# One expert at a time on both column halves of TensorE, with 4 MB weight loads and sums kept in PSUM, in the expert layer of a one-layer diffusion backbone

## The reference, cut to what matters

```python
combine = jnp.sum(one_hot(top_idx, 32) * softmax(top_vals)[..., None], axis=1)
def expert(acc, xs):
    wu, bu, wd, bd, g = xs                  # wu (1024, 2048), wd (1024, 1024)
    gu = x @ wu + bu
    gate, up = gu[:, :1024], gu[:, 1024:]
    gate = jnp.minimum(gate, 7.0); up = jnp.clip(up, -7.0, 7.0)
    y = ((up + 1.0) * gate * sigmoid(1.702 * gate)) @ wd + bd
    return acc + g[:, None] * y, None
xs = xs + gt_f * acc ;  y_out = rmsnorm(xs, g_final)
```

## Time and profile before

| | |
|---|---|
| time, median of 3 runs | 1152.67 us (1152.51 to 1154.61) |
| profiled execution | span 1150.5 us; its time with what lies around the span isn't listed, the median run is 2.2 us above the span |
| TensorE matmul busy | 1054.2 us, 92% of the span |
| VectorE, ScalarE, GpSimd busy | 331.5, 176.1, 55.6 us |
| DMA | 459.15 MB, mean 399 GB/s over the span |
| DMA in 40 slices of 28.8 us | 309 376 247 334 385 289 311 281 419, then 400 to 429 to slice 39, last 212 GB/s |

### The profile page before, as it was taken

How to read it: one execution, slowest core, us unless ns; L and a number is a source line. 1 busy time by engine, 2 the same in 40 slices (tenths; PEclk the granted TensorE clock), 3 DMA queues, 4 the chain that set the end, 5 groups by cost and what they waited for, 6 DMA issues and landing times.

```text
span 1150.5 us, 13989 instructions
## 1 busy us (share of the span) xinstructions
PE 1054.2 (92%) x5718; PEld 518.3 (45%) x5718; DVE 331.5 (29%) x613; ACT 176.1 (15%) x319; POOL 55.6 (5%) x92
## 2 busy tenths in 40 slices
PE   7999999999999999989899998989898989898986
PEld 6987699834434343424243433333434333343422
DVE  4675877412213112111120202120212121212125
ACT  4453145401101010101010101010101010000011
POOL 5050000300000000000000000000000000000000
PEclk9999999999999999999999999999999999999999
DMA  9988987799999999999999999999999999999995
GB/s 309 376 247 334 385 289 311 281 419 428 427 400 428 427 429 428 428 428 429 428 429 428 428 428 428 428 429 428 429 428 428 429 428 428 428 427 424 421 420 212
DMA packets 58658, 459.15 MB, mean 399 GB/s; under 512 B 4804, under 2 KB 17160, under 8 KB 28056
## 3 DMA queue, kind: packets, MB, share of 16 engines
q1 hardware_dynamic: 57256, 455.12, 95.6%
q0 software_dynamic: 1168, 2.81, 1.0%
q10 hardware_dynamic: 192, 0.66, 0.2%
HBM read 456.99 MB, written 1.57 MB: 399 GB/s over the span
## 4 chain that ended last, share of the span: by engine, by line
PE 61%; DMA 33%; DVE 2%; SPq 2%; issue 1%; ACT 1%; DVEq 0%; ACTq 0%
DMA ring<-in_w_down_dram 30%; PE ps L1862 17%; PE ps L1877 10%; PE ps L1798 6%; PE ps L1751 5%; PE ps L1762 5%; PE ps L1447 3%; DMA ring<-in_w_in_dram 2%; PE ps L1897 2%; PE ps L1791 1%; PE ps L1778 1%; DMA ring<-in_w_ada_dram 1%; PE ps L1504 1%; PE ps L1505 1%; PE ps L1673 1%
## 5 line engine op out<-in xcount | busy, mean ns | idle before, releaser
L1862 PE MATMUL ps<-ring,arena 128*64 128x512 f32 x1664 | 364.5, 593 | 14.6 <-DMA ring<-in_w_up_dram 14.5
L1877 PE MATMUL ps<-ring,arena 128*64 128x512 f32 x896 | 210.8, 626 | 54.6 <-DMA ring<-in_w_down_dram 54.6
L1862 PEld LDWEIGHTS ps<-ring,arena 128*64 128x64 f32 x1664 | 121.0, 137 | 241.6 <-issue 239.2
L1877 PEld LDWEIGHTS ps<-ring,arena 128*64 128x64 f32 x896 | 72.5, 144 | 192.6 <-issue 173.5
L1305 DVE TENSOR_TENSOR arena<-ps,arena 128x512 f32<-128x512 f32 x64 | 44.3, 692 | 299.0 <-PE ps L1762 299.0
L1286 DVE TENSOR_SCALAR arena<-ps 128x512 f32<-128x512 f32 x32 | 20.6, 686 | 255.7 <-PE ps L1862 217.4
L1798 PE MATMUL ps<-ring,arena 128*64 128x512 f32 x368 | 81.1, 594 | 1.4 <-DVE arena L1288 0.7
L1751 PE MATMUL ps<-arena 128*128 128x128 f32 x512 | 63.7, 282 | 0.0
L1751 PEld LDWEIGHTS ps<-arena 128*128 128x128 f32 x512 | 61.7, 196 | 2.8 <-issue 2.8
L858 ACT ACTIVATE arena<-arena 128x512 f32<-128x512 f32 x32 | 19.6, 629 | 268.5 <-DVE arena L1286 268.4
L1762 PE MATMUL ps<-arena 128*128 128x512 f32 x128 | 57.8, 594 | 1.2 <-ACT arena L871 1.2
(11 more groups left out here) (281 smaller groups left out, 955.4 us busy)
## 6 DMA issues: line engine op xcount, KB each, us to landing
ring<-in_w_up_dram SPq DMA_DIRECT2D x127, 2048.0 KB, 26.9
ring<-in_w_down_dram SPq DMA_DIRECT2D x63, 2048.0 KB, 23.0
ring<-in_w_ada_dram SPq DMA_DIRECT2D x16, 1024.0 KB, 10.4
ring<-in_w_ada_dram SPq DMA_DIRECT2D x16, 512.0 KB, 10.1
ring<-in_w_in_dram SPq DMA_DIRECT2D x16, 512.0 KB, 9.5
ring<-in_w_in_dram SPq DMA_DIRECT2D x8, 1024.0 KB, 7.4
ring<-in_w_out_dram SPq DMA_DIRECT2D x4, 1024.0 KB, 6.8
ring<-in_w_pb_dram SPq DMA_DIRECT2D x2, 1024.0 KB, 8.2
```

The costliest lines, as they stand in the source:

```text
L1862: ins = mm(ps[CAP * a:CAP * a + CAP, n, :], xgT[:, h, kk, CAP * a:CAP * a + CAP], w[a][:, n * HALF:(n + 1) * HALF], start=False, stop=(kk ...
L1877: ins = mm(ps[CAP * a:CAP * a + CAP, YB + n, :], hT[:, f, CAP * a:CAP * a + CAP], w[a][:, n * HALF:(n + 1) * HALF], start=(f == 0), stop=( ...
```

## The change

1. **One expert on both column halves.** The same 64 tokens are the stationary operand on both halves. A row block's 2048 up columns are dealt out as `(g p j)` with j = 8: half h takes columns 4h to 4h+3 of every 8. So `up_row` reads 4 adjacent float32 of each 8 as moving operand, and gate and up of one expert fill banks 0 and 1. `down_rows` gives each half 512 of the 1024 output columns, in one bank (`YB`).
2. **Loads.** An up load is 4 MB (half an expert, 32 KB a partition), a down load 4 MB (32 KB a partition). There are four up buffers (`QUADS`: two for even, two for odd experts) and one down buffer, `down_buf`, in the arena; 20 MB together. The first eight loads of experts 0 and 1 are 2 MB halves, and `down_buf` is first filled once the router's logits are done. Expert 31's down weights go in five pieces over expert 30's first up buffer.
3. **Order of loads in the loop.** After expert e-1's down product: down(e), second up half of e+2, first up half of e+3.
4. **Sums stay in PSUM.** The residual x is put into banks 4 to 7 by `inject`, `gated` (VectorE) multiplies the down result with the ffn gate, and `scatter` adds on top with two 64-row products a token tile (rows 0 to 63 give bank 4+2t, rows 64 to 127 bank 5+2t). `acc`, `y_out`, `add_acc`, the copies of x back to SBUF (`x_back`) and `keep_busy` go. The down biases enter as a first scatter.
5. `gather` works for one pair's tokens, a half of the channels in each of two steps, and reads every fourth column of `h2`.
6. The mixing slots are renumbered one for one; slots 6 and 7 come free with the branch products (`br_done`, L1676) and are loaded then.

The core of the diff (the mixing plan, declarations and the handling of further rounds are left out):

```diff
-    w_up_v = A_w_up[0].rearrange("e (c p j) n -> e p c (j n)", p=P, j=2)
-    w_down_v = A_w_down[0].rearrange("e (c p j) n -> e p c (j n)", p=P, j=4)
+    w_up_v = A_w_up[0].rearrange("e (c p j) n -> e p c (j n)", p=P, j=4)
+    w_down_v = A_w_down[0].rearrange("e (p j) n -> e p (j n)", p=P)
...
+                first_free = [(O_done, 1), (kv_stored, 32), (unit_ready, 24), (unit_ready, 24), (br_done, KB),
+                              (unit_ready, 28), (unit_ready, 32), (out_done, KB)]
+                order = [(0, 0, 0), (0, 0, 1), (0, 1, 0), (0, 1, 1), (1, 1, 1), (1, 0, 1), (1, 0, 0), (1, 1, 0)]
...
+                if r == 0:
+                    sp.wait_ge(logit_done, 2)
+                for h in range(2):
+                    down_part(0, 4 * h, 4 * h + 4, down_loaded[h])
+                for h in range(2):
+                    sp.wait_ge(moe_free, R + freed(0) + h + 1)
+                    up_part(2, 0, h)
+                up_whole(2, 0, 1, R + freed(0) + 4)
+                up_whole(3, 1, 0, R + freed(1) + 2)
+                up_whole(3, 1, 1, R + freed(1) + 4)
+                down_whole(1, R + freed(1) + 6)
+                up_whole(4, 0, 0, R + freed(2) + 2)
+                def steady(e, parity, at):
+                    down_whole(e, at + 6)
+                    up_whole(e + 2, parity, 1, at + 4)
+                    up_whole(e + 3, 1 - parity, 0, at + 8)
...
+            def gated(g, used):
+                dve.wait_ge(moe_free, used)
+                dve.wait_ge(scat_done, g + 1)
+                for t in range(2):
+                    V.tensor_tensor(yg[:, t, :], ps[:, YB, :], gate_rows[:, t, :], ALU.mult).then_inc(yg_ready, 1)
...
-                                 h2[:, t, 2 * P * (j // 2) + j % 2:2 * P * (j // 2 + 1):2],
-                                 oh[:, t, :], start=(t == 0), stop=(t == 1))
+                        ins = mm(ps[:, bank, j * P:(j + 1) * P], h2[:, t, HALF * c + j:HALF * (c + 1):4],
+                                 oh[:, t, :], start=(t == 0), stop=(t == 1))
...
+            def up_row(e, kk):
+                place, a = (e // 2 + 1) % 2, e % 2
+                w = up_chunk(e, kk // 4)[:, kk % 4, :].rearrange("q (g p j) -> q g p j", g=2, j=8)
+                for half in range(2):
+                    for h in range(2):
+                        ins = mm(ps[CAP * h:CAP * h + CAP, half, :].rearrange("q (p j) -> q p j", j=4),
+                                 xgT[:, place, kk, CAP * a:CAP * a + CAP], w[:, half, :, 4 * h:4 * h + 4],
+                                 start=False, stop=(kk == KB - 1))
...
+            def scatter(g, done, each=0, last=False):
+                pe.wait_ge(woT_ready, g + 2)
+                for t in range(2):
+                    pe.wait_ge(yg_ready, g * 2 + (3 + t))
+                    for n in range(2):
+                        rows = slice(CAP * n, CAP * n + CAP)
+                        ins = mm(ps[:, XB + 2 * t + n, :], woT[rows, t, :], yg[rows, t, :], start=False, stop=last)
...
+            def step(e, g, n, laps, loads, r):
+                up(e, g, laps, r, r == 0 and e == 0)
+                if e:
+                    down(e - 1, g - 1, loads)
+                turn_hidden(g)
+                if e < E - 2:
+                    pe.wait_ge(u_read, g + 2)
+                    gather(n, e % 2, 0)
+                if e or r == 0:
+                    scatter(g - 1, scat_done)
```

More of the change, by code:

```diff
@@ L393, in mixing_chunk @@
                     sp.wait_ge(*give_back(PLAN[b][:3]))
-                if slot > 9:
+                if kind == "out" and k >= 2:
                     sp.wait_ge(O_done, 1)
@@ L906, in experts, with run @@
-                hT_out(Q, hT_last)
-                y_out(used - DNC)
-                woT_out(Q)
+                        step(FIRST_BODY + h, g0 + h)
+                for e in range(E - FIRST_BODY, E):
+                    step(e, R + e)
+                woT_out(R + E - 1)
+            def run(r):
+                act.wait_ge(last_scat, 2 * r)
+                experts(r)
+                act.wait_ge(last_scat, 2 * (r + 1))
             experts(0)
-            further_rounds(act, read_flags(act), experts)
+            further_rounds(act, read_flags(act), run)
@@ L1335, in _ @@
+                for e in range(E - FIRST_BODY, E):
+                    step(e, R + e, r * PAIRS + e // 2 + 2, slice(e // 2 + 1, e // 2 + 2), N + freed(e))
+                gated(R + E - 1, N + PIECES)
             dve.wait_ge(count_done, 1)
-            link(V.tensor_reduce(misc[:, 9:10], ps[:, 5, 0:E], AX.X, ALU.max))
+            link(V.tensor_reduce(misc[:, 9:10], ps[:, YB, 0:E], AX.X, ALU.max))
             for r in range(ROUNDS):
@@ L1806, in up_first, with up @@
+            def up(e, g, laps, r, first=False):
+                R = r * E
+                if not first:
+                    pe.wait_ge(xg_ready, g + 2 if e < E - 1 else g + 1)
+                    bias(g)
                 for kk in range(KB):
+                    c = kk // 4
                     if kk % 4 == 0:
[L1808 to L1813 removed]
@@ new lines, in up @@
+                    if kk % 4 == 2 and (e, c) in HALVED:
+                        per = 2 if c == e % 2 else 1
+                        pe.wait_ge(up_loaded[2 * (e % 2) + c][1], 16 * (r * per + HALVED[e, c] + 1))
+                    if first:
+                        if kk == 0:
+                            pe.wait_ge(xg_ready, 1)
+                        if kk == 2:
+                            pe.wait_ge(h2_ready, 4)
+                            gather(1, 1, FIRST[1])
+                            totals()
+                        if kk == 4:
+                            pe.wait_ge(xg_ready, 2)
+                            inject(1, 0)
+                        if kk == 5:
+                            pe.wait_ge(wo_ready, 1)
+                            for t in range(2):
+                                ins = tp(ps[:, TB, t * P:(t + 1) * P], wo[:, t, :, :].rearrange("p a b -> p (a b)"),
+                                         ident[:, :])
+                            ins.then_inc(woT_done, 1)
+                    elif kk == 3 and e:
+                        turn_weights(g - 1)
@@ L1947, in experts @@
-                scatter(Q)
-                down_by_block(Q, at(n0 + PC), hT_last, LAST_YB, lambda: turn_weights(Q), 16 * (r + 1))
-            pe.sem_inc(woT_done, 1)
+                        step(FIRST_BODY + h, g0 + h, n0 + h // 2, laps0 + 16 * (h // 2),
+                             [(down_loaded[0], loads0 + 16 * h, 8)], r)
+                for e in range(E - FIRST_BODY, E):
+                    step(e, *fixed(r, e), r)
+                turn_weights(R + E - 1)
+                down(E - 1, R + E - 1, fixed(r, E))
```

884 lines of the change are left out of this document (352 added, 532 removed).

## The result

The changed kernel takes **1163.7 us** (median of 4 runs, 1163.09 to 1165.1) against 1152.59 us for the kernel before, run beside it (4 runs, 1152.01 to 1154.61): ratio 1.0096, 95% interval 1.0082 to 1.011. The sign of the forecast (1156.2, slower) is right and its range (1146 to 1165) holds the time; the forecast's own range, 1153 to 1160, does not. What went wrong is what rival 4 describes, a dearer gather. The profiled execution took 1163.09 us, its span is 1161.3. All medians are of fast executions; one execution of experiment 1's kernel took 1551.34 us at a granted clock of 0.65 and is not counted.

What follows compares the result with a forecast made beforehand. Loads bound the expert stage, with TensorE trailing at the end: down(2) at 302.2 + 2.2 + 796.1 gives down(29) at 1100.5, last down product 1141.8, span 1154.0, plus 2.2 gives 1156.2 us; range 1146 to 1165.

Steps and rivals of the forecast that it cites:

- rival 4: Gather's stationary operand at step 4 gets dearer: up to 7.5 us over four gathers, 1163.7 us; chance 0.05.
- Gather in TensorE's turn: Expert loop: one expert's gather takes 1.88 us of a 25.8 us turn, with no cost for step 4.
- The start: Expert stage up to the issue of down(2): first up product at 226.3 us, down(2) issued at 302.2.
- the first activation: Expert 0, no down product to hide its activation: 4.75 us, to 248.9 us.
- the slow clock: After TensorE's idle time at expert 0's activation, the lower granted clock costs 1.7 us.
- The rate: Loop loads with 32 KB runs: 432 GB/s, so 343.9 MB from down(2) to down(29) take 796.1 us.
- The wait in the turn: Loop: TensorE waits 3 us a turn for the down load just issued, last in line.
- The end: After down(29) lands at 1100.5 us, TensorE trails with 40.5 us of work plus 0.8 clock loss, to 1141.8.
- The tail: After the last down product: 6.2 us to the second root, then 5.95 to the span's end.
- rivals 5 and 6: Half-height scatters don't overlap: 1162.6 us, chance 0.03; up product's moving operand reads slower: 10% adds 5.5 us, chance 0.03.
- 3 by the 432: Rival on loads: 32 KB runs bring nothing or are cut again, 428 GB/s, +7.4 us, 1163.6 us; chance 0.09.
- Rival 1: Loop loads: longer runs pay more, 436 GB/s, 7.3 us less, 1148.9 us, faster; chance 0.28.

Runs made afterwards that it cites:

- experiment 1: Changed kernel with token rows stored in the gather's reading order, so its operand runs at unit step, result the same: 1158.65 us, ratio 1.005.
- experiment 3: Changed kernel with gather operand at step 8 instead of 4, the first gather waiting for all token rows: 1165.67 us (one run).
- experiment 6: Changed kernel with every 4 MB load issued as two of 2 MB with 16 KB runs, each half waited for at first use: 1168.7 us.
- experiments 4 and 5: On the changed kernel: expert 31's second up half ahead of expert 29's down weights, 1174.93 us; 4 MB of unread loads added at the end, 1163.57 us.
- experiment 7: Changed kernel with last loads reordered from expert 24 on, down(29) ahead of expert 31's first up half, no byte added: 1157.02 us.

## Why the prediction was right in sign and short in size

The span came out 7.3 us above the forecast's 1154.0. By its own steps:

- **Gather in TensorE's turn: the step that failed.** The forecast carried 1.88 us over from the earlier trace rows and wrote of the step of 4 "I take none". At a step of 4 it is 3.8 us, and with the step taken away (experiment 1) it is 1.9 again. Its reason was that step 2 costs no more than unit step; that is true (196 and 192 ns) and says nothing of step 4, where the price sets in at once (experiment 3). The SBUF rule that the forecast cited (the Trainium skill, "SBUF — State Buffer", note on cachelines in section Door 1) has its threshold at two hits on a 16-byte line, which is the one that the four steps show; its remark that a step of 4 float32 is still free is not borne out (329 ns against 192). With 7.5 us for four gathers the sum gives rival 4's 1163.7; that this equals the measured median is partly luck, as the next points cancel. So is experiment 1's down(2) at 302.25: TensorE got through its start 1.0 us sooner than the forecast's sum (bias of up(1) at 253.93 against 254.9) and was 1.0 slower over the two turns behind it. Of the 7.5 us experiment 1 gave 5.1 back; the rest is accounted for only in part.
- **The start.** down(2) was issued at 307.71, 5.5 late. Four gathers are 7.5 by the forecast's price. Against them: the first activation stood in the way for 3.3 us and not 4.75, since the table load ran at 242.96 under the up product; and of the 1.7 us set for the slow clock behind it only about 0.4 came (6.63 us from 251.16 to 257.79, where the same work takes 6.23 in the turn at 532.40), since it didn't lengthen the gather at step 4. The turns themselves were a little longer than the sum had them.
- **The rate.** 432 in the windows, as worked out; experiment 6 gives 428 for halved loads and runs. But from 307.71 + 2.2 to the wait's end at 1108.39 the 343.9 MB took 798.5 us, which is 430.7 GB/s over the whole way: 2.4 us more. Only 0.4 us of that can be placed, at the start (414 GB/s from 309.9 to 320 us); the 425 GB/s of 300 to 500 us count the gap before the issue, and from 320 us on it is 431. So down(29) was 5.5 + 2.4 = 7.9 us late.
- **The wait in the turn.** 1.0 us instead of 3, the direct mirror of the gather's 1.9.
- **The end.** From down(29)'s start to the end of the last down product 41.9 us, forecast 41.3. That TensorE's trail and not the loads sets it, and that down(29) is its head, is shown by experiments 4 and 5; experiment 7 moves down(29) and the end by the same 6.7 us. The tail was 11.0 instead of 12.2: 0.6 - 1.2 = -0.6. Sum 7.9 - 0.6 = 7.3 us.
- **Half-height scatter, up product at its new places, loads ahead:** 1.91 us, 13.9 us and a first wait only for down weights; rivals 5 and 6 are out, and 3 by the 432. Rival 1 is out too: 432 GB/s over 550 us, with 434 only in the 50 us from 1050 to 1100.

What the change itself is worth follows from experiment 1: with the gather mended it is still 5.9 us slower than the kernel before. The change's order of loads puts those for two turns ahead in front of the down weights that TensorE wants next; turning that round near the end gave 6.7 us, and halving three loads at the start, together with one swap, gave 3.2. The larger loads with their longer runs gave 7.4 us of rate at most.

## What to carry to other kernels

Read the load of the stationary operand on its own: when a layout change alters the step between its elements, look up the step's price beyond what the trace shows, because here steps 1 and 2 told nothing of step 4; a copy that is written once can take the permutation, so that the operand of 512 weight loads is dense. In this stream, bound by loads, the order near the end was worth as much as the rate: put first what starts the longest trail of compute, and try it by moving one transfer in front of another, which adds no byte. And a price that the loop covers is still paid while the loop isn't level with its loads, at both ends.

## What the runs showed of the hardware that was not expected

- LDWEIGHTS of 128x128 float32: 192, 196, 329, 335 ns at steps of 1, 2, 4, 8 elements. At the lower clock level the load at unit step took up to 337 ns, while the one at step 4 never passed 332, with the clock at 0.50 in 253 to 256 us too. So at this step something other than TensorE's clock limits, and a gather of 16 took 4.00 us at 222.88 and at 231.24, at full clock, and at 251.65, where the clock was 0.64 over it.
- VectorE's reads of PSUM at a step of 4 float32 cost nothing: 743 ns for a 128x512 product, 744 at unit step (experiment 1 and kernel after).
- A wait of 2.9 us in the loop was followed by a granted clock of 0.50 (experiment 1, 986 to 990 us) and one of 3.0 by 1.00 (1044 to 1047 us), so the length of the wait alone doesn't decide it; with waits of 1.0 us a turn (kernel after) the clock stayed at 1.00 from 300 to 1100 us.
